# Four transformer layers on one core: the first model's output projection in two halves by rows, and the pieces of the modulation sums placed anew

## The chip, the cores and the metric

The kernel runs on one core of one Trainium2 chip. The metric is the device time of one execution in microseconds. TensorE is called PE here, VectorE DVE, ScalarE ACT, GpSimd POOL and SyncE SP, as in the profile.

## The reference

Two models run one after the other on 256 tokens of width 1024, each with two layers. Every layer adds a gated mixer and a gated feed-forward part to the tokens. The gates, shifts and scales of a layer are six vectors of width 1024, from one matrix product of a condition with a matrix of 1024 x 6144:

```python
c_act = jax.nn.silu(c)
mod = c_act @ ada_w[layer] + ada_b[layer]
sh_m, sc_m, gt_m, sh_f, sc_f, gt_f = jnp.split(mod, 6)
h = modulate(rms_norm(x, norm_mix_g[layer]), sh_m, sc_m)
x = x + gt_m * hybrid_mixer(h, ...)
h = modulate(rms_norm(x, norm_ffn_g[layer]), sh_f, sc_f)
x = x + gt_f * f(h)
# hybrid_mixer of the first model, after z = h @ w_in and the split into columns
rg_out = rg_lru(causal_depthwise_conv(rg_x), ...) * jax.nn.gelu(rg_gate)        # 512 wide
gla_out = rms_norm(gla_chunked(q, k, v, log_f)) * jax.nn.silu(g)                # 4 heads of 128
return jnp.concatenate([rg_out, gla_out], axis=-1) @ w_out
```

The feed-forward part is a gated unit of width 2816 in layer 0 of the first model and eight experts, two chosen for each token, in layer 1. The second model's mixer has a latent attention and a gated recurrent memory (mLSTM) with branch projections and an output projection; its feed-forward part has a short convolution. All is in float32.

## The kernel before

Tokens lie feature-major: x and h are eight blocks of 128 features by 256 tokens. Each engine runs one list of instructions written out by hand, and semaphores join them. Weights come in units of 1 MB through a ring of six slots; SP loads them in one fixed order (`unit_plan`), and the load of a unit waits until the unit that held its slot is used. A product of float32 precision is made of three in the rounded type float32r: the weights and the tokens are each split in a high part (ACT copies it with rounding, `high` in line 1429) and a low part (DVE subtracts, `low` in line 1950), and PE adds high x high, low x high and high x low in PSUM (`project_split`). The output projections and a few others are plain float32 matmuls (`project`), 128 instructions for the whole of `w_out`. The high part of the mixer's tokens is `mix_h_hi`. In the first model's mixer the eight input units are rgx 0 and 1, flow, q, k, v 0 and 1, gate 0 and 1, g 0 and 1; the second model's has vm 0 and 1 among them.

The modulation sums are made beside that. A layer's matrix is cut into 24 pieces of 128 rows by 2048 columns, 1 MB each. POOL loads a piece into a slot of `ada_in`; DVE multiplies it by its 128 conditions and adds it to one of the three accumulators `ada_acc` (`ada_piece`, line 1900, 2.35 us for a piece, 1.2 us for a first one). When all eight pieces of an accumulator are in, PE sums over partitions, one matmul with one column of ones for each 128 outputs (`modulation`, line 639): a layer has 48 such blocks, 16 in each accumulator, and each is two instructions. The third slot of `ada_in` is at the same time `mix_h_hi`, so that in layer 0 after the first eight pieces, in the last layer, and for the first pieces of the others, two slots are in use (`ada_plan`); the third is loaded only when the unit g 1 has been used.

Where a piece stands in DVE's queue is written by hand. In `mixer1` (line 2023) `late(li, a, b)` does a pieces in layer 0 and b in layer 1; those of layer 0 are the last 16 of its own 24, those of layer 1 belong to the second model's first layer, whose other 16 are done beside the experts. In `mixer2` the second model's last layer's pieces are done: 18 in the mixer, six in the convolution stage.

The end of `mixer1` on PE: the head products (o) into banks 6 and 7, the modulation columns, the sums of squares of the heads, and `project_out`, which waits for the whole concatenated input `ycat_ready`. DVE makes that input in h: the recurrent half as one product, each head half by a reciprocal, a scaling and two products with the silu of g. Then DVE adds bank by bank to x (`residual`, line 2154), ACT squares x, PE sums (`norm_sum`), ACT takes the root and DVE the reciprocal (`norm`), and the next stage begins. In layer 0 the low parts of the first feed-forward units w1 and w3 (`split_low`) stand on DVE before the residual, in `mixer2` those of u1 and u3.

## Time and profile before

| | |
|---|---|
| median of 3 runs | 2437.72 us (2433.67 to 2438.7) |
| the profiled execution | 2435.66 us |
| its span in the profile | 2433.9 us |
| PE busy, share | 2261.0 us, 93% |
| DVE busy, share | 1774.9 us, 73% |
| ACT busy, share | 1228.7 us, 50% |
| granted PE clock, mean | 0.95 |

The stages by the trace, in us from the start: start and first norm until 56, first mixer 56 to 230, feed-forward 230 to 421, second mixer 435 to 574, routing and experts 577 to 1415, second model's first mixer 1445 to 1720, convolution stage 1723 to 1925, last mixer 1940 to 2212, last convolution stage 2215 to 2413, output until 2434. A stage ends for the next when the last x is written and normed. A wait is shown with the instruction that ended it; a wait "by DVEq" or "ACTq" is one for a semaphore that the queue of that engine raised after an instruction had settled.

### The profile page before, as it was taken

What the parts mean: (1) busy time and instruction counts of PE and PEld (TensorE: products, weight loads), DVE (VectorE), ACT (ScalarE), POOL (GpSimd) and SP (SyncE); (2) the same over time, 40 slices, a digit from 0 to 9 for tenths busy, and PEclk for the clock granted to TensorE, in tenths of its full rate; (3) what the DMA queues carried; (4) which work ended last, traced back from release to release, by engine and by line L of the source; (5) the groups of instructions that cost most, each with busy time, mean ns of one, the idle gap of its engine ahead of it and who ended that gap; (6) DMA issues with size and microseconds to landing.
All of it is one profiled execution on the core that took longest, in us unless ns stands there. A gap on an engine that the chain in (4) does not pass through costs nothing.

```text
span 2433.9 us, 33478 instructions
## 1 busy us (share of the span) xinstructions
PE 2261.0 (93%) x13955; PEld 2020.0 (83%) x13955; DVE 1774.9 (73%) x1894; ACT 1228.7 (50%) x1338; POOL 55.2 (2%) x101
## 2 busy tenths in 40 slices
PE   3948999888999999999999989999999999999997
PEld 2847999877888888888888877878899988888997
DVE  5864876766898989999899856676677563556675
ACT  2612343633777677676767734522455444324553
POOL 1000000000000000000000000000000000000000
PEclk9968999977999999999999979989999898999998
DMA  8862987344999999999999925855466263234551
GB/s 279 272 247 70 339 301 277 123 144 185 355 353 379 355 370 369 352 378 357 371 368 352 355 66 146 278 189 191 156 211 203 73 159 104 87 133 138 181 192 51
DMA packets 338896, 578.55 MB, mean 238 GB/s; under 512 B 48083, under 2 KB 208811, under 8 KB 326451
## 3 DMA queue, kind: packets, MB, share of 16 engines
q1 hardware_dynamic: 324041, 474.36, 57.3%
q0 software_dynamic: 13824, 100.67, 10.9%
q8 instruction: 112, 1.84, 0.3%
q10 hardware_dynamic: 873, 1.31, 0.2%
q14 instruction: 46, 0.37, 0.1%
HBM read 575.26 MB, written 1.05 MB: 237 GB/s over the span
## 4 chain that ended last, share of the span: by engine, by line
PE 79%; DVE 10%; ACT 4%; DMA 3%; issue 2%; SPq 1%; DVEq 0%; ACTq 0%; POOL 0%
PE bank L557 78%; DVE w_low L1890 2%; ACT arena L1414 2%; DVE arena L1898 1%; DMA ring<-in_w_in 1%; DVE ada_acc L1898 1%; SPq L445 1%; DMA ada_in<-in_ada_w 1%; ACT L1414 1%; PE bank L1195 1%; DVE arena L1890 1%; ACT mix_hi L1414 1%; DVE arena L1980 1%; DVE arena L2331 1%; DVE arena L2091 1%
## 5 line engine op out<-in xcount | busy, mean ns | idle before, releaser
L1890 DVE TENSOR_TENSOR w_low<-ring,moe_w_hi 128x2048 fp32r<-128x2048 f32 x264 | 594.5, 2284 | 14.4 <-ACT moe_w_hi L1414 13.9
L1414 ACT ACTIVATE moe_w_hi<-ring 128x2048 fp32r<-128x2048 f32 x264 | 505.4, 1917 | 155.6 <-DMA ring<-in_moe_w 93.7
L557 PE MATMUL bank<-mix_h_hi,mix_hi 128*128 128x256 f32 (+2 forms) x848 | 255.7, 301 | 44.0 <-DVE w_low L1890 30.8
L557 PE MATMUL bank<-moe_w_hi,hx_hi 128*128 128x512 f32 (+1 forms) x768 | 285.2, 378 | 2.0 <-DVE hx_low L1890 2.0
L557 PE MATMUL bank<-moe_w_hi,hx_low 128*128 128x512 f32 (+1 forms) x768 | 284.1, 376 | 0.0
L557 PE MATMUL bank<-h_hi,w_hi 128*128 128x256 f32 x1056 | 263.5, 287 | 16.9 <-ACT h_hi L1414 11.3
L557 PE MATMUL bank<-h_hi,w_low 128*128 128x256 f32 x1056 | 262.4, 285 | 0.0
L557 PE MATMUL bank<-mix_h_hi,w_low 128*128 128x256 f32 (+2 forms) x848 | 250.1, 295 | 0.0
L557 PE MATMUL bank<-h_low,mix_hi 128*128 128x256 f32 (+2 forms) x848 | 244.7, 294 | 0.0
L1414 ACT ACTIVATE arena<-bank 128x512 f32<-128x512 f32 (+2 forms) x174 | 91.3, 525 | 265.3 <-PE bank L557 256.9
L1898 DVE SCALAR_TENSOR_TENSOR ada_acc<-ada_in,c_col,ada_acc 128x2048 f32<-128x2048 f32 x84 | 197.0, 2348 | 31.7 <-DMA ada_in<-in_ada_w 26.5
L557 PEld LDWEIGHTS bank<-h_hi,w_hi 128*128 128x128 f32 x1056 | 202.7, 192 | 18.7 <-issue 12.1
L557 PEld LDWEIGHTS bank<-mix_h_hi,mix_hi 128*128 128x128 f32 (+2 forms) x848 | 168.6, 199 | 53.1 <-issue 47.0
L557 PEld LDWEIGHTS bank<-h_hi,w_low 128*128 128x128 f32 x1056 | 204.1, 193 | 0.0
L557 PE MATMUL bank<-w_low,hx_hi 128*128 128x512 f32 (+1 forms) x768 | 194.1, 378 | 0.0
L1890 DVE TENSOR_TENSOR w_low<-ring,w_hi 128x2048 fp32r<-128x2048 f32 x66 | 148.8, 2289 | 38.9 <-ACT w_hi L1414 38.9
L557 PEld LDWEIGHTS bank<-moe_w_hi,hx_hi 128*128 128x128 f32 x768 | 145.1, 189 | 30.5 <-DVE hx_low L1890 2.2
L557 PEld LDWEIGHTS bank<-mix_h_hi,w_low 128*128 128x128 f32 (+2 forms) x848 | 169.0, 199 | 1.3
L557 PEld LDWEIGHTS bank<-moe_w_hi,hx_low 128*128 128x128 f32 x768 | 145.2, 189 | 28.0
L557 PEld LDWEIGHTS bank<-h_low,mix_hi 128*128 128x128 f32 (+2 forms) x848 | 165.2, 197 | 2.4 <-DVE h_low L1898 1.0
L1890 DVE TENSOR_TENSOR w_low<-ring,mix_hi 128x1024 fp32r<-128x1024 f32 (+2 forms) x128 | 138.7, 1126 | 35.4 <-ACT mix_hi L1414 27.8
L1414 ACT ACTIVATE w_hi<-ring 128x2048 fp32r<-128x2048 f32 x66 | 123.1, 1903 | 81.6 <-DMA ring<-in_ffn_w_up 63.2
(190 smaller groups left out, 4396.0 us busy)
## 6 DMA issues: line engine op xcount, KB each, us to landing
ring<-in_moe_w SPq DMA_DIRECT2D x264, 1024.0 KB, 6.2
ada_in<-in_ada_w POOLq DMA_DIRECT2D x96, 1024.0 KB, 7.5
ring<-in_w_in SPq DMA_DIRECT2D x56, 1024.0 KB, 5.4
ring<-in_ffn_w_up SPq DMA_DIRECT2D x44, 1024.0 KB, 7.1
ring<-in_ffn_w SPq DMA_DIRECT2D x33, 1024.0 KB, 5.8
ring<-in_ffn_w_down SPq DMA_DIRECT2D x22, 1024.0 KB, 4.9
ring<-in_w_out SPq DMA_DIRECT2D x16, 1024.0 KB, 5.3
ring<-in_w_br_mla SPq DMA_DIRECT2D x4, 1024.0 KB, 4.9
```

The costliest lines, as they stand in the source:

```text
L445: sp.dma_start(dst, src).then_inc(s["params"], 16)
L557: ins = nc.tensor.matmul(out, lhsT, rhs, start=start, stop=stop, skip_group_check=shared)
L1195: ins = nc.tensor.transpose(bank[2 * (q % 2)][:, i * P:(i + 1) * P], MS["hid"][:, i * P:(i + 1) * P], ident)
L1414: return nc.scalar.activation(out, in_, f, **kw)
L1890: return nc.vector.tensor_tensor(out, a, b, op)
L1898: return nc.vector.scalar_tensor_tensor(out, a, sc, b, op0, op1)
L1980: settle(nc.vector.reciprocal(region(2048, T), region(2304, T)))
L2091: settle(nc.vector.reciprocal(M1["rec"], M1["rec"]))
L2331: settle(nc.vector.reciprocal(M2["hstd"][:, sl], M2["hstd"][:, sl]))
```

## The change

- The first model's output projection is done in two halves by rows of `w_out`: for all four banks first the four blocks of the recurrent half (now in `gg`), then the four of the heads (now in `aa`). `ycat_ready` is raised three times, after the recurrent half and after each head half.
- The unit g 1 is projected behind the heads' products instead of before them; its silu stands behind the heads' square roots on ACT.
- `mix_h_hi` lies in the first accumulator instead of the third slot of `ada_in`. Three slots are in use throughout, and the pieces go accumulator by accumulator: 0, 1, 2 in the first model, 1, 2, 0 in the second.
- Pieces are placed anew. Layer 0's 16: 2, 1, 1 as before, then 2 behind the split of gate 1, 1 behind that of g 0, 3 behind the recurrent half, and 2, 2, 1, 1 beside the residual (before: 2, 1, 1, 2, 1, 6, 3). Layer 1 does 12 of the next 24 (2, 1, 1, 2, 1, 1 and 2, 1, 1, 0 beside the residual; before 3, 2, 2, 1 there), the experts 12 (before 16). In the second model's first mixer all 24: 4, six steps of the attention, five of the memory, 1, 1, and 2, 2, 2, 1 beside the residual.
- Modulation columns: in layer 0, 16 before the head sums and 16 after the norm's sum; in layer 1 all 32 before the mixer.
- Of the first two units of a mixer the second is split behind the norm's root (high part) and behind the tokens' low parts (low part). The high parts of vm 0 and 1 go behind later copies of ACT. The constant of the recurrence gate is made earlier.

The core of the diff; hunks are named by engine, and what is left out repeats these edits:

```diff
@@ placement of the buffers
-        ada_acc = sb("ada_acc", [P, ADA_SLOTS, SLOT])
-        ada_in = sb_at("ada_in", [P, ADA_SLOTS, SLOT])
+        ada_acc = sb_at("ada_acc", [P, ADA_SLOTS, SLOT])
+        ada_in = sb("ada_in", [P, ADA_SLOTS, SLOT])
...
-        mix_h_hi = rounded("mix_h_hi", [P, KB, T], "ada_in", 2 * SLOT)
+        mix_h_hi = rounded("mix_h_hi", [P, KB, T], "ada_acc")
...
-            return (layer, m % KB, m // KB) if layer == 0 else (layer, m // ADA_SLOTS, m % ADA_SLOTS)
+            return layer, m % KB, ((0, 1, 2) if layer < 2 else (1, 2, 0))[m // KB]
@@ gpsimd
-                slot, _, there = ada_places[n]
-                if there is not None:
-                    pool.wait_ge(s["ada_used"], there + 1)
-                if n in (ADA_PER_LAYER + 2, 2 * ADA_PER_LAYER + 2):
-                    pool.wait_ge(s["units_used"], plan[("g", n // ADA_PER_LAYER - 1, 1)][2] + 1)
+                slot = n % ADA_SLOTS
+                if n >= ADA_SLOTS:
+                    pool.wait_ge(s["ada_used"], n - ADA_SLOTS + 1)
@@ tensor
-            def gate_modulation():
+            def ffn_modulation():
+                need("ada_done")
                 fill(7)
-                modulation(7, 5 * KB, MODS)
+                modulation(7, 4 * KB, 5 * KB)
+                fill(0)
+                modulation(0, 5 * KB, MODS)
...
-                project_bank(("g", li, 1), 4)
-
                 need("scores_sb", 2)
                 need("states_sb")
...
+                project_bank(("g", li, 1), 4)
                 if li == 0:
                     need("ada_done")
-                fill(2)
-                modulation(2, 2 * KB, 3 * KB)
+                    fill(2)
+                    modulation(2, 2 * KB, 4 * KB)
                 need("headsq_sb", 2)
...
-                modulation(2, 3 * KB, MODS if li else 5 * KB)
-                project_out("wout", li, (2, 3, 5, 4))
+                gg = M1["gg"].rearrange("p (b t) -> p b t", b=4)
+                heads = M1["aa"].rearrange("p (b t) -> p b t", b=4)
+                banks = (2, 3, 5, 4)
+                need("ycat_ready")
+                for j, b in enumerate(banks):
+                    fill(b)
+                    arrive(("wout", li, j))
+                    w = slot_view(("wout", li, j), KB, 256)
+                    for i in range(2):
+                        for kb in range(4):
+                            mm(bank[b][:, i * T:(i + 1) * T], w[:, kb, i * P:(i + 1) * P], gg[:, kb, :],
+                               start=(i == 0 and kb == 0), stop=False, shared=True)
+                for j, b in enumerate(banks):
+                    w = slot_view(("wout", li, j), KB, 256)
+                    for hh in range(2):
+                        if j == 0:
+                            need("ycat_ready")
+                        for i in range(2):
+                            for head in (hh, hh + 2):
+                                mm(bank[b][:, i * T:(i + 1) * T], w[:, 4 + head, i * P:(i + 1) * P],
+                                   heads[:, head, :], start=False, stop=(head == 3), shared=True,
+                                   inc="wout_psum" if i and head == 3 else None)
+                    owed.append(1)
...
+            fill(7)
+            modulation(7, 2 * KB, MODS)
             mixer1(1)
@@ scalar: norm (for a mixer's two first units), mixer1, mixer2
-                for key in mixer:
-                    high(key)
+                if mixer:
+                    high(mixer[0])
                 need("norm_sum")
                 tell(func(region(2304, T), bank[1][:, 0:T], ACT.Sqrt, scale=1.0 / DM, bias=EPS), "norm_std", 1)
+                if mixer:
+                    high(mixer[1])
...
+                need("c8_ready")
+                func(small[:, 4:8], small[:, 4:8], ACT.Exp, scale=-1.0)
                 need("lf_abs")
...
-                need("c8_ready")
-                settle(func(small[:, 4:8], small[:, 4:8], ACT.Exp, scale=-1.0))
...
+                high(("g", li, 0))
                 need("rgchain_v")
...
-                for g, b, ahead in ((1, 6, ("km", li, 1)), (2, 7, ("vm", li, 0)), (3, 3, ("vm", li, 1))):
...
                 tell(func(M2["qr"], bank[5][:, :], ACT.Copy), "qr_sb", 5)
+                high(("vm", li, 0))
...
+                high(("vm", li, 1))
                 for half, b in enumerate((2, 4)):
@@ vector: mixer1
+                if li:
+                    modulation(1, 2 * KB, MODS, 7)
+                lam = v[:, PACK1["lam"]:PACK1["lam"] + 4]
+                tell(stt(small[:, 4:8], lam, -1.0, lam, ALU.mult, ALU.max), "c8_ready")
                 nc.vector.memset(M1["sc"], 0.0)
-                late(li, 2, 0)
+                late(li, 2, 2)
...
                 low(("k", li, 0))
-                late(li, 1, 0)
+                late(li, 1, 1)
                 low(("v", li, 0))
-                late(li, 1, 0)
+                late(li, 1, 1)
...
-                late(li, 2, 0)
                 low(("gate", li, 0))
...
-                late(li, 1, 0)
                 low(("gate", li, 1))
+                late(li, 2, 2)
+                low(("g", li, 0))
+                late(li, 1, 1)
...
-                low(("g", li, 0))
-                late(li, 6, 0)
...
-                late(li, 3, 0)
-                if li == 0:
-                    ada_finish(0)
...
-                need("outgate_sb", 2)
-                hh1 = h[:, 0:4, :].rearrange("p k t -> p (k t)")
-                settle(tt(hh1, M1["mu"], M1["gg"], ALU.mult))
+                tell(tt(M1["gg"], M1["mu"], M1["gg"], ALU.mult), "ycat_ready")
+                late(li, 3, 1)
+                if li == 0:
+                    ada_finish(0, 2)
+                    modulation(0, 2 * KB, 4 * KB, 2)
...
-                tell(ins, "ycat_ready")
-                modulation(li, 2 * KB, MODS if li else 5 * KB, 2)
+                    tell(ins, "ycat_ready")
                 if li == 0:
                     split_low("w", 0, 0)
-                residual((2, 3, 5, 4), 16, "wout_psum", (0, 0, 0, 0) if li == 0 else (3, 2, 2, 1))
+                residual((2, 3, 5, 4), 16, "wout_psum", lambda j: late(li, (2, 2, 1, 1)[j], (2, 1, 1, 0)[j]))
+                if li == 0:
+                    ada_finish(0)
@@ vector: mixer2, experts, convolution stage
-                    ada_next(1)
+                    if step < 6:
+                        ada_next(1)
...
                 gated_heads(1)
+                ada_next(1)
                 gated_attention(2, 5)
                 gated_attention(3, 1)
+                ada_next(1)
...
                 split_low("u", li, 0)
-                residual((0, 5, 3, 7), 16, "wout_psum")
+                residual((0, 5, 3, 7), 16, "wout_psum", lambda j: ada_next((2, 2, 2, 1)[j]))
+                if li == 0:
+                    ada_finish(3)
...
-                            if part == 1 and c in (0, 3):
+                            if part == 1 and (c == 0 or (c == 3 and e % 2 == 0)):
                                 ada_piece(next(pieces))
...
-                    if f % 3 == 1:
-                        for n in itertools.islice(pieces, 1):
-                            ada_piece(n)
```

## Rows read from the trace of the kernel before

**Rows 1.** first part of the page, busy time by engine.

```profile
...
PE 2261.0 (93%) x13955; PEld 2020.0 (83%) x13955; DVE 1774.9 (73%) x1894; ACT 1228.7 (50%) x1338; POOL 55.2 (2%) x101
...
```

**Rows 2.** busy time by stretch, then granted clock, DMA share, GB/s.

```profile
...
605.00:1405.00 800.00, 799.59 (x3905) 664.33 (x3906) 720.41 (x473) 563.64 (x402) 7.92 (x15) 1.00 0.99 359
153.60:166.60 13.00, 12.85 (x88) 12.06 (x88) 9.62 (x15) 0.62 (x2) 1.05 (x2) 0.89 0.47 166
1508.00:1522.00 14.00, 8.47 (x17) 4.12 (x18) 4.66 (x7) 7.69 (x12) 0.00 (x0) 0.76 0.13 41
...
```

**Rows 3.** waits of PE, 100 to 232 us: sum, times, longest.

```profile
...
PE bank L557 <- DVE w_low L1890: 23.6, 2, 18.4
PE bank L557 <- DVEq L1916: 7.1, 1, 7.1
PE bank L557 <- DVEq L1885: 6.1, 1, 6.1
...
```

**Rows 4.** groups of DVE, 104 to 190.3 us: busy, mean | idle before.

```profile
...
L1898 DVE SCALAR_TENSOR_TENSOR ada_acc<-ada_in,c_col,ada_acc 128x2048 f32<-128x2048 f32 x9 | 21.2, 2351 | 17.7 <-DMA ada_in<-in_ada_w 16.7 <-DVE arena L1898 0.7 <-DVE arena L1890 0.2
L1890 DVE TENSOR_TENSOR w_low<-ring,mix_hi 128x1024 fp32r<-128x1024 f32 x6 | 7.1, 1220 | 0.4 <-DVE arena L2100 0.2
L2141 DVE RECIPROCAL arena<-arena 128x512 f32<-128x512 f32 x2 | 6.7, 3349 | 0.0
...
```

**Rows 5.** waits of PE, 1445 to 2120 us.

```profile
...
PE bank L557 <- ACTq L1409: 11.6, 2, 5.9
PE bank L557 <- DVE w_low L1890: 7.7, 7, 3.0
PE bank L912 <- DVEq L1885: 6.7, 3, 4.0
...
```

**Rows 6.** DVE in order of time: start, length, what [idle before].

```profile
...
116.59 6.55 DVE L2091 RECIPROCAL arena<-arena 128x1024 f32<-128x1024 f32 x1
...
155.93 3.00 DVE L1898 SCALAR_TENSOR_TENSOR arena<-arena,small,bank 64x128 f32<-64x128 f32 x8
...
171.17 2.35 DVE L1898 SCALAR_TENSOR_TENSOR ada_acc<-ada_in,c_col,ada_acc 128x2048 f32<-128x2048 f32 x1 [6.75 <-DMA ada_in<-in_ada_w]
...
220.14 0.88 DVE L1898 SCALAR_TENSOR_TENSOR x<-bank,mod,x 128x256 f32<-128x256 f32 x2 [6.03 <-PE bank L557]
...
1716.28 0.88 DVE L1898 SCALAR_TENSOR_TENSOR x<-bank,mod,x 128x256 f32<-128x256 f32 x2 [6.03 <-PE bank L557]
...
```

**Rows 7.** groups of PE, 190.4 to 220.15 us.

```profile
...
L557 PE MATMUL bank<-h,ring 128*128 128x256 f32 x128 | 29.7, 396 | 6.1 <-DVEq L1885 6.1
...
```

**Rows 8.** GpSimd's issues in order of time.

```profile
...
162.25 0.53 POOL L535 DMA_DIRECT2D ada_in<-in_ada_w  x1 [10.95 <-DVE ada_acc L1898]
...
```

**Rows 9.** PE in order of time.

```profile
...
229.59 0.55 PE L557 MATMUL bank<-h_hi,w_hi 128*128 128x256 f32 x1 [4.35 <-ACT h_hi L1414]
...
435.03 0.55 PE L557 MATMUL bank<-mix_h_hi,mix_hi 128*128 128x256 f32 x1 [6.61 <-ACT mix_h_hi L1414]
...
```

**Rows 10.** groups of PE, 524 to 540.05 us.

```profile
...
L557 PE MATMUL bank<-const,ada_acc 128*128 128x1 f32 x64 | 12.5, 330 | 0.0
L557 PE MATMUL bank<-arena,const 128*128 128x512 f32 x4 | 3.8, 1096 | 0.0
```

**Rows 11.** busy time by stretch, as Rows 2.

```profile
...
529.50:539.50 10.00, 10.00 (x49) 10.00 (x47) 9.59 (x8) 0.60 (x1) 0.00 (x0) 0.50 0.12 42
421.30:424.80 3.50, 3.50 (x34) 3.50 (x33) 2.65 (x7) 1.33 (x3) 0.00 (x0) 1.00 0.56 168
...
```

**Rows 12.** groups of PE, 540.05 to 570.8 us.

```profile
...
L557 PE MATMUL bank<-h,ring 128*128 128x256 f32 x128 | 30.6, 405 | 0.4 <-issue 0.4
...
```

**Rows 13.** ACT in order of time.

```profile
...
1501.81 2.00 ACT L1414 ACTIVATE mix_hi<-ring 128x1024 fp32r<-128x1024 f32 x2 [10.08 <-DMA ring<-in_w_in]
...
1701.61 1.91 ACT L1414 ACTIVATE w_hi<-ring 128x2048 fp32r<-128x2048 f32 x1 [2.20 <-DMA ring<-in_ffn_w_up]
...
```

**Rows 14.** waits of PE, 2215.3 to 2413.1 us.

```profile
...
PE bank L557 <- DVE w_low L1890: 4.8, 3, 3.0
...
...
```

More of the change, by code:

```diff
@@ L207, in unit_plan @@
     return order, plan, earlier, split
-def ada_plan():
-    places, count, holder = [], [0] * ADA_SLOTS, [-3, -2, -1]
-    for n in range(4 * ADA_PER_LAYER):
-        layer, m = divmod(n, ADA_PER_LAYER)
-        two = (layer == 0 and m >= KB) or (layer in (1, 2) and m < 2) or layer == 3
-        slot = min(range(2 if two else ADA_SLOTS), key=lambda i: holder[i])
-        count[slot] += 1
-        places.append((slot, count[slot], holder[slot] if holder[slot] >= 0 else None))
-        holder[slot] = n
-    return places
 def two_blocks(nc, d, out):
     order, plan, earlier, split = unit_plan()
-    ada_places = ada_plan()
     MOE0, MOE_SLOT = plan[("moe", 0, 0)][2], plan[("moe", 0, 0)][0]
@@ L1555, in mixer1 @@
                 tell(ins, "rgchain_m")
-                high(("g", li, 0))
                 need("kend_psum")
@@ L1569, in mixer1 @@
                          "headsq_sb")
+                for half in range(2):
+                    need("headsum_psum")
+                    tell(func(M1["ostd"][:, half * 512:(half + 1) * 512], bank[half][:, :], ACT.Sqrt,
+                              scale=1.0 / P, bias=EPS), "headstd_sb", half)
                 for half, b in enumerate((5, 4)):
@@ L1573, in mixer1 @@
                          "outgate_sb", b)
-                for half in range(2):
-                    need("headsum_psum")
-                    tell(func(M1["ostd"][:, half * 512:(half + 1) * 512], bank[half][:, :], ACT.Sqrt,
-                              scale=1.0 / P, bias=EPS), "headstd_sb", half)
             def mixer2(li):
@@ L1601, in mixer2 @@
                      "cqstd", 0)
-                for g, b, ahead in ((1, 6, ("km", li, 1)), (2, 7, ("vm", li, 0)), (3, 3, ("vm", li, 1))):
+                for g, b in ((1, 6), (2, 7), (3, 3)):
                     conv_last_tap(li, v, qk, g, b)
-                    high(ahead)
+                    if g == 1:
+                        high(("km", li, 1))
                 need("m_rows")
@@ L1973, in split_h, with norm @@
                         ALU.add, ALU.subtract).then_inc(s["h_lo"], 1)
-            def norm(scale, out, inc, first=False, mixer=()):
-                for key in mixer:
-                    low(key)
+            def norm(scale, out, inc, columns=None, mixer=()):
+                if mixer:
+                    low(mixer[0])
                 need("norm_std")
                 settle(nc.vector.reciprocal(region(2048, T), region(2304, T)))
-                if first:
-                    modulation(0, 0, 2 * KB, 0)
+                if columns:
+                    modulation(*columns)
                 for kb in range(KB):
@@ L2537, in moe_dense @@
                 dve.sem_inc(s["moe_hid"], 4)
-                pieces = iter(range(2 * ADA_PER_LAYER + 8, 3 * ADA_PER_LAYER))
+                pieces = iter(range(2 * ADA_PER_LAYER + 12, 3 * ADA_PER_LAYER))
                 done = [0]
                 for e in range(EXPERTS):
-                    for j in range(2):
-                        ada_piece(next(pieces))
+                    for n in itertools.islice(pieces, 2):
+                        ada_piece(n)
                     for c in range(MOE_CHUNKS):
@@ L2565, in conv_ffn @@
                 t1, t2 = vcol[:, 4 + 2 * li, :], vcol[:, 5 + 2 * li, :]
-                pieces = iter(range(4 * ADA_PER_LAYER - 6, 4 * ADA_PER_LAYER) if li == 0 else ())
                 c0 = f0 - F0["conv0"]
@@ L2601, in _ @@
             start()
-            norm(scale_a[:, 0, :], h, "norm_mul", first=True, mixer=(("rgx", 0, 0), ("rgx", 0, 1)))
+            norm(scale_a[:, 0, :], h, "norm_mul", columns=(0, 0, 2 * KB, 0), mixer=(("rgx", 0, 0), ("rgx", 0, 1)))
             split_h(0, mix_h_hi, 0)
+            low(("rgx", 0, 1))
             rope()
             mixer1(0)
-            norm(scale_a[:, 1, :], h, "norm_mul")
-            modulation(0, 5 * KB, MODS, 7)
+            norm(scale_a[:, 1, :], h, "norm_mul", columns=(0, 4 * KB, 5 * KB, 7))
+            modulation(0, 5 * KB, MODS, 0)
             split_h(1, h_hi, 24)
@@ L2612, in _ @@
             split_h(2, mix_h_hi, 0)
+            low(("rgx", 1, 1))
             mixer1(1)
@@ L2620, in _ @@
             split_h(4, mix_h_hi, 0)
+            low(("cq", 0, 0))
             mixer2(0)
@@ L2627, in _ @@
             split_h(6, mix_h_hi, 0)
+            low(("cq", 1, 0))
             mixer2(1)
```

37 lines of the change are left out of this document (16 added, 21 removed).

## The prediction, before the changed kernel was run

> **What bounds the kernel now.** I began with the page's first part: PE is busy for 93% of the span, 173 us short of all of it, and DVE for 73% [rows 1]. The sum of busy time by stretch then says where those 173 us can lie. In the 800 us of the experts PE is busy for 799.59 us at a granted clock of 1.00, while DVE works for 720 us [rows 2]: fewer pieces there free DVE and nobody waits for it. So only PE's idle stretches and its half-clock stretches are to be had, and the view of waits names them. From 100 to 232 us, the first layer's mixer, PE waits 23.6 us for splits by DVE (one wait of 18.4), 7.1 us for the end of the pieces and 6.1 us for the gated heads [rows 3]: 37 us of some 130, and a short wait before the gate unit besides. In that stretch DVE's nine multiply-and-add pieces cost 21.2 us and another 16.7 us in which DVE itself waits for their transfers [rows 4]; they stand in the queue ahead of the split that the second g unit needs and ahead of the heads. In the second model PE waits 11.6 us in two equal waits for ACT, 6.7 us in three for the attention weights and 7.7 us for splits in the convolution stage [rows 5].
>
> **First layer, mixer: a gain of 28 us.** Pieces are re-placed, not saved: 16 stay between the first norm and the feed-forward stage. In the new queue 2 stand after the second gate split and 1 after the first g split. Before that point DVE loses about 1.4 us (the second rgx split, 2 x 1.2 us [rows 4], now stands behind the norm, which itself starts 1.2 us sooner) and wins 4.7 us from the two pieces taken out ahead of the gate split, so PE's short wait before the gate unit goes. DVE reaches the reciprocal chain at about the old moment, 116 us; the reciprocal alone is 6.55 us [rows 6], the chain 9.3, so 125.3. Then, with no piece in between, masks 1.7, split of g1 2.4 [rows 4], states 4.4 (3.0 of them the row at 155.93 [rows 6], the rest four copies ahead of it) and their settling: 134, where before it was 159. PE does the g0 unit meanwhile and idles for about 9 us, then does the heads' products and g1, which before, in the other order, took PE 12.9 us from 153.6 [rows 2], some 2 of it at half clock as now: 147.7 by my reckoning, states 134 and 13.7 us on. DVE in that time makes the first half of the concatenated input (2.5 + 2.4 + 1.2 us: 140.5) and three pieces, 147.7. PE then does 16 modulation columns, 3.6 us, and the head sums, 1.8 us: 153.3. The projection is 29.7 us for 128 instructions [rows 7]; its first half, 14.8 us, runs while DVE does the two head halves, each a reciprocal of 3.35 us [rows 4] and 1.5 us around it, after the square roots: 163.2. So PE would end near 183, not 220. But DVE is late then: two splits of w1 and w3 bring it to 169.6, and six pieces (14.1 us) and four residual pairs (1.1 us each) follow. Three transfers stand ready; the fourth must be fetched again. The slowest of these stood 8.9 us between issue, 162.25, and use, 171.17 [rows 8, 6], which would leave DVE waiting for 4 us over the tail; the other bound is nothing. I take 3, nearer the row. The last x is then written at about 191.3 against 220.14 + 0.9 [rows 6]. From there to the first matmul of the feed-forward stage was 8.6 us [rows 6, 9]; 16 columns on a slow PE stand before the scales now, 1.5 us more: 201.5 against 229.6, so 28. Bounds: 33 if no transfer is late, 20 if each of the last six costs what the longest did.
>
> For that transfer the Trainium skill, DMA: Bandwidth & Descriptors, section Bandwidth, gives 6.15 us for 1 MB from GpSimd's queue. By it DVE would hardly wait in this tail, the gain would be about 31 us, and with the other tail the sum 59 us in place of 55; the 8.9 us of [rows 8, 6] speak against it here, though they hold the issue too.
>
> **Second layer, mixer: 14 us.** All 32 modulation columns leave the end of the mixer, where 64 instructions of one column took 12.5 us and the head sums 3.8 us [rows 10], and stand behind the norm's sum, where PE idles for 6.61 us before its first projection [rows 9]. At a granted clock of 1.00, 34 such instructions fit in 3.5 us; from 529.5 to 539.5 us, at 0.50, there were 49 in 10 us [rows 11]. So 64 take from 6.6 to 13.1 us, and the start of the mixer moves from -1.5 us (PE does not go cold) to +7; I take +2.5, as the first half of them run warm. Then as in the first layer: states at about 514, products and g1 until 527.5, head sums until 529.3, projection 27.6 us at full clock: 556.9, against 570.7 before (30.6 us for it [rows 12]). The heads (534 and 539) are ready before PE has ended the first half at 543. Four pieces beside the residual fit into DVE's waits. Bounds 6 to 18 us. Without the split by rows this layer would start the projection at 539, so 10 of the 14 us hang on it; in the first layer DVE's tail swallows that difference.
>
> **Second model, both layers: 8 us each before the scores, 2 and 1 elsewhere.** ACT holds the copy that PE's rotation waits for behind the high part of a value unit whose weights arrive late: ACT idles 10.08 us for them [rows 13]. The diff puts those two high parts behind the copy; what they release is needed only 5 and 12 us later, so the wait that ends at 1513.53 goes. Each such wait is 5.8 us [rows 5], and the stretch behind it, 1508 to 1522, had a mean clock of 0.76 [rows 2], some 2.5 us of loss. That makes 8.3 in each layer; bounds 5 to 8.5. In the first of them the three pieces at the end of the attention loop go: the wait of 4.0 us [rows 5] has one piece of 2.35 us right in front of the normalisation, so 2.4 are saved. The norms gain 0.5 and 1.2 us. Together 11 and 10 us.
>
> **Tail of the second model's first layer: a loss of 11 us.** Seven pieces move behind the split of the first up units. That split waits for weights which SP may load only after the last branch unit is used: ACT begins u3's high part at 1701.61 [rows 13], DVE ends its low part at 1705.9. Before, four residual pairs followed, the last at PE's pace, from 1716.28 [rows 6] to 1717.2. Now 7 x 2.35 + 4 x 1.1 = 21 us follow on DVE, and a transfer that is 1 us late: 1728. Bounds 6 (part of the pieces hidden in a way I miss) to 16 us (three late transfers). What is given back: the convolution stage has no pieces, and its splits keep PE waiting 4.8 us in the last layer, which has none, against 7.7 us [rows 5, 14]: 3 us.
>
> **Hidden at nothing.** Four fewer pieces in the experts: PE's full queue covers them. The order j by j makes each piece wait for the one before it on its own engine, and DVE's settling is 0.2 us at most, between pieces that rarely touch. GpSimd's queue has three slots throughout and no longer waits for the g unit; only its transfers come earlier. The high part of the tokens changes place, not work. SP's queue is not changed.
>
> **Waits that are added.** PE's queue now stops three times for the concatenated input, for the product of the recurrent half and for each head half; behind the second stop stand all the second-half matmuls, and DVE's residual waits for those. In my times (140.5, 158 and 163 against 153, 168 and 168) none of the three is reached late. In the first layer PE also waits for two thirds of the pieces before its 16 columns, with the head sums behind it; that is 147.7, the moment at which g1 ends, and each us by which the three pieces are late there delays head sums, square roots and projection alike, though DVE's tail hides some 8 us of it. ACT waits for the second head half before it rounds w1 and w3; DVE's low parts stand behind that. ACT's exponential of the gate constant moves next to that of the log gate, so that two table loads go; what they held up is the gate split, already counted.
>
> **The sum.** 28 + 14 + 11 - 11 + 3 + 10 = 55 us. The profiled execution took 2435.66 us, its span 2433.9. So 2380.7, and for the shown runs, whose median lies 2 us above that execution, 2382 us. About 0.2%, 5 us, is what a measurement of this kernel tells from no change.
>
> **Rivals.** (1) PE's clock: the long row of one-column matmuls and the new 9 us gap before the heads' products cost double, with the projections beginning at half clock: +10, 2392 us, chance 0.14. For it speaks the clock of 0.50 in [rows 11]. (2) The tails: every refilled transfer takes 9 us or more because up to four ring loads go at the same time; first mixer 20, second model's tail -16: 2395 us, 0.13. (3) The value units' weights come too late for the new places as well, so PE stops at the values, not at the rotation: 11 to 16 us of the second model are lost, 2396 us, 0.07. (4) The gain is larger: no transfer late and no cold start of the second mixer, 33 + 18 + 11 - 10 + 3 + 10 = 65: 2372 us, 0.12. (5) Slower than before: one mechanism, the pieces' transfers. 16 pieces stay on DVE's path in the first mixer; if each waited 3.5 us more than my tails allow, the 55 us would be gone, and above it the kernel is slower: 2441 us at 3.7. Before, the nine pieces of [rows 4] made DVE wait 16.7 us, 1.9 each, with two slots in place of three; chance 0.02. (6) The split by rows does nothing, since PE reaches the first half only when the heads are done: 10 us of the second layer are lost, 2392 us, 0.05; the head sums, which PE must do first, leave 10 us for DVE, so little speaks for it. My forecast, 2376 to 2388, holds the rest, 0.47. The range 2367 to 2398 reaches to the first four cases. Faster 0.96, same 0.02, slower 0.02.
>
> **What would show it.** After: the wait of 18.4 us gone and one of about 9 us before the heads' products; DVE's last residual of layer 1 near 191 us and PE idle in front of it; the expert stage 40 us earlier and unchanged in length; no wait for ACT before the rotation; in the second model's first layer a PE wait of over 10 us before the convolution stage. Wrong if the chain before 116 us moves, or if weights, not pieces, set the tails.

## The result, and the profile after

| | before | after |
|---|---|---|
| median | 2435.69 us (4 runs) | 2395.49 us (4 runs, 2391.27 to 2400.01) |
| the profiled execution, its span | 2435.66, 2433.9 us | 2391.27, 2389.5 us |

The ratio is 0.9835, 95% interval 0.9811 to 0.9858: about 40 us faster, and 44.4 us between the profiled executions. Forecast were 2382 us (range 2367 to 2398) and 55 us. The direction and the places where the time moves were forecast; 11 us of the amount did not come between the profiled executions, and 15 by the medians. The profiled execution after is the fastest of its four, and no trace shows where the 4 us between the two figures lie. To see where the 11 us are missing, I cut both traces at the first matmuls of the stages. The last column is the prediction's term.

| stage, by PE | before | after | gained | forecast |
|---|---|---|---|---|
| start to the feed-forward stage | 229.6 | 206.8 | 22.8 | 28 |
| to the router (second mixer) | 348.0 | 337.2 | 10.8 | 14 |
| routing and experts | 842.1 | 840.9 | 1.2 | 0 |
| second model: norm, mixer, to its output projection | 268.7 | 259.5 | 9.2 | 11 |
| output projection to convolution stage | 34.7 | 46.6 | -11.9 | -11 |
| convolution stage and last mixer | 492.1 | 480.7 | 11.3 | 3 + 10 |
| last stage | 218.7 | 217.9 | 0.9 | 0 |

The page's first part shows the sum, where [rows 1] stood before: PE has lost 6 us of busy time and 38 us of idle time.

```profile
PE 2254.6 (94%) x13955; PEld 2016.7 (84%) x13955; DVE 1776.4 (74%) x1895; ACT 1223.7 (51%) x1334; POOL 53.7 (2%) x101
```

The waits of PE from 100 to 207 us answer to [rows 3]. Both waits for splits, the one for pieces and the one for the gated heads are gone; 7.3 us ahead of the heads' products stand in their place (the view names no releaser; PE's queue stands there for the states, which DVE settles at 134.7).

```profile
PE bank L542 <- issue: 7.3, 1, 7.3
PE bank L542 <- ACT arena L1417: 4.4, 3, 2.3
PE bank L542 <- ACTq L1414: 2.0, 1, 2.0
PE bank L542 <- DVEq L1895: 0.7, 1, 0.7
```

What the idle time costs is seen in PE's groups from 135 to 160.7 us and in the granted clock of the same stretch: the 40 small matmuls of the heads take 10.5 us at a clock of 0.50, and g 1 begins at 0.50 as well. Before, the 40 took 5.8 us, from 518.07 to 523.83.

```profile
L542 PE MATMUL bank<-arena 64*128 64x64 f32 (+1 forms) x40 | 10.5, 439 | 7.3 <-issue 7.3
...
L542 PE MATMUL bank<-const,ada_acc 128*128 128x1 f32 x32 | 4.4, 272 | 0.0
L542 PE MATMUL bank<-arena,const 128*128 128x512 f32 x4 | 3.8, 1096 | 0.0
```

```profile
135.00:145.50 10.50, 10.50 (x41) 9.14 (x41) 9.72 (x10) 0.60 (x1) 0.96 (x1) 0.50 0.01 2
145.50:152.70 7.20, 7.20 (x51) 7.20 (x51) 2.35 (x1) 0.60 (x1) 1.12 (x3) 0.80 0.91 341
```

PE in order of time: the same ten microseconds again in the second mixer, then the two starts that answer to [rows 9] and to the convolution stage. In the wait of 6.56 us PE stands for ACT's square of x, and ACT for DVE, which has pieces to do first.

```profile
135.00 10.52 PE L542 MATMUL bank<-arena 128*128 128x128 f32 x40 [7.28 <-issue]
...
206.80 0.58 PE L542 MATMUL bank<-h_hi,w_hi 128*128 128x256 f32 x1 [0.67 <-DVEq L1895]
...
489.99 10.52 PE L542 MATMUL bank<-arena 128*128 128x128 f32 x40 [7.28 <-issue]
...
1681.48 2.08 PE L542 MATMUL bank<-arena,const 128*128 128x256 f32 x4 [6.56 <-ACT arena L1417]
...
1690.92 0.55 PE L542 MATMUL bank<-h_hi,w_hi 128*128 128x256 f32 x1 [3.46 <-ACT h_hi L1417]
```

DVE in order of time, first mixer and second model's first: it idles 9.14 us before the heads and 9.71 us before the split of u1, and in both tails works through pieces while PE has ended. Only one transfer is late in the first tail, by 1.68 us.

```profile
157.04 0.18 DVE L1898 TENSOR_TENSOR mod<-bank,vcol 128x16 f32<-128x16 f32 x1 [9.14 <-PE bank L542]
...
186.52 2.35 DVE L1906 SCALAR_TENSOR_TENSOR ada_acc<-ada_in,c_col,ada_acc 128x2048 f32<-128x2048 f32 x1 [1.68 <-DMA ada_in<-in_ada_w]
...
195.70 0.87 DVE L1906 SCALAR_TENSOR_TENSOR x<-bank,mod,x 128x256 f32<-128x256 f32 x2
...
1655.80 2.29 DVE L1898 TENSOR_TENSOR w_low<-ring,w_hi 128x2048 fp32r<-128x2048 f32 x1 [9.71 <-ACT w_hi L1417]
...
1683.65 0.87 DVE L1906 SCALAR_TENSOR_TENSOR x<-bank,mod,x 128x256 f32<-128x256 f32 x2
```

### The profile page after: what moved, and what is told of

The parts are those of the page before. It is cut to its first block, busy times and chain, and to the rows that moved or that the text cites. A ratio compares the mean times of both kernels' runs of the same rounds, so it can differ in the third digit from the quotient of the medians.

```text
span 2389.5 us, 33477 instructions
## 1 busy us (share of the span) xinstructions
PE 2254.6 (94%) x13955; PEld 2016.7 (84%) x13955; DVE 1776.4 (74%) x1895; ACT 1223.7 (51%) x1334; POOL 53.7 (2%) x101
## 4 chain that ended last, share of the span: by engine, by line
PE 84%; DVE 8%; ACT 3%; DMA 2%; issue 2%; SPq 1%; DVEq 0%; ACTq 0%; POOL 0%; POOLq 0%
PE bank L542 82%; ACT arena L1417 1%; DVE w_low L1898 1%; SPq L432 1%; DMA ring<-in_w_in 1%; DVE ada_acc L1906 1%; PE bank L1196 1%; DVE arena L1906 1%; DMA ada_in<-in_ada_w 1%; DVE arena L1898 1%; ACT mix_hi L1417 1%; DVE arena L2344 1%; DVE arena L2101 1%; DVE h L1906 0%; DMA ring<-in_ffn_w_up 0%
## 5 line engine op out<-in xcount | busy, mean ns | idle before, releaser
L1898 DVE TENSOR_TENSOR w_low<-ring,moe_w_hi 128x2048 fp32r<-128x2048 f32 x264 | 594.4, 2285 | 14.6 <-ACT moe_w_hi L1417 14.2
L1906 DVE SCALAR_TENSOR_TENSOR ada_acc<-ada_in,c_col,ada_acc 128x2048 f32<-128x2048 f32 x84 | 197.3, 2348 | 19.5 <-DMA ada_in<-in_ada_w 12.6
L542 PEld LDWEIGHTS bank<-mix_h_hi,mix_hi 128*128 128x128 f32 (+2 forms) x848 | 167.0, 197 | 22.8 <-issue 14.1
L1906 DVE SCALAR_TENSOR_TENSOR arena<-bank,vcol,arena 128x255 f32<-128x255 f32 (+3 forms) x252 | 111.0, 481 | 79.2 <-ACT arena L1417 75.1
L542 PEld LDWEIGHTS bank<-moe_w_hi,hx_low 128*128 128x128 f32 x768 | 145.1, 189 | 27.9
```

Source lines behind the costliest of these rows:

```text
L542: ins = nc.tensor.matmul(out, lhsT, rhs, start=start, stop=stop, skip_group_check=shared)
L1898: return nc.vector.tensor_tensor(out, a, b, op)
L1906: return nc.vector.scalar_tensor_tensor(out, a, sc, b, op0, op1)
```

## Experiments

Two theories for the missing 11 us. **Clock:** PE idles before the heads' products and pays for it at half clock. **Transfers:** refilled pieces come late. Rivals for single terms: the split by rows does nothing; the edit of vm 0 and 1 does nothing. Ratios below are to the kernel before, run on the same chip.

### e1: the output projection not split by rows

```diff
-                need("ycat_ready")
+                need("ycat_ready", 3)
                 for j, b in enumerate(banks):
...
-                        if j == 0:
-                            need("ycat_ready")
```

> The changed kernel, but PE waits for the recurrent half and both head halves before the first matmul of the output projection; the rest is unchanged. If the split by rows hides the two head halves, as the prediction has it: in the first layer the projection starts at 170.2 in place of 160.4 us and the last x comes 4 to 5 us later (DVE's tail hides the rest), in the second it starts at about 519.6 in place of 509.3, 10 us later: 14 to 15 us slower than the changed kernel, a ratio to the kernel before near 0.989. If the split does nothing, because PE reaches the projection only when the heads are done: no difference, 0.983. If DVE's tail hides the whole of it in the first layer: 10 us, 0.987.

Measured 2409.11 us, ratio 0.9907 (0.9888 to 0.9927), some 17 us above the changed kernel's ratio, where 14 to 15 were expected. The waits of PE from 100 to 575 us show the two stops:

```profile
PE bank L542 <- DVEq L1891: 19.8, 2, 10.2
```

From first projection to feed-forward stage the first layer took 156.3 us in place of 150.6, and the second, to the router, 142.2 in place of 129.1. The second costs 13 us, not 10, since PE runs slower behind the wait: the 128 matmuls took 30.1 us at a mean clock of 0.93, in place of 27.8 at 1.00. The split does what it was given, and a little more.

### e3 and e5: the value units' edit alone, on the kernel before

```diff
@@ scalar (e3 and e5)
-                for g, b, ahead in ((1, 6, ("km", li, 1)), (2, 7, ("vm", li, 0)), (3, 3, ("vm", li, 1))):
+                for g, b in ((1, 6), (2, 7), (3, 3)):
...
                 tell(func(M2["qr"], bank[5][:, :], ACT.Copy), "qr_sb", 5)
+                high(("vm", li, 0))
...
+                high(("vm", li, 1))
@@ vector (e5 only)
-                low(("vm", li, 0))
                 conv_taps(v, qk, 3, 3)
-                low(("vm", li, 1))
+                low(("vm", li, 0))
...
+                low(("vm", li, 1))
                 need("atok_psum")
```

> The kernel before, with one edit of the change alone: the high parts of the units vm 0 and vm 1 on ACT behind the copies of the rotated query part and of the values, in both layers of the second model. By the prediction each layer wins 5.8 us of wait and 2.5 us of half clock behind it: 16 to 17 us faster than before, a ratio of 0.993. If only the waits go and the clock behind them stays low: 11 to 12 us, 0.995. If the weights come too late for the new places as well, PE waits at the values instead and 0 to 5 us are won, 0.998 to 1.000.

e3: 2436.03 us, ratio 1.0014 (1.0001 to 1.0026). All three expectations missed: not even the wait's 11 us came. From the first projection to the next stage the first of the two layers took 280.7 us in place of 277.7, the second 272.1 in place of 274.7. The waits of PE from 1500 to 1560 us and DVE's order of time say why for the first:

```profile
PE bank L557 <- ACTq L1411: 6.5, 1, 6.5
PE bank L557 <- DVEq L2376: 3.8, 1, 3.8
```

```profile
1506.74 2.36 DVE L1893 TENSOR_TENSOR w_low<-ring,mix_hi 128x1024 fp32r<-128x1024 f32 x2 [4.54 <-ACT mix_hi L1414]
1509.02 2.68 DVE L1901 SCALAR_TENSOR_TENSOR arena<-bank,vcol,arena 128x255 f32<-128x255 f32 x6
```

The low part of vm 0 stands on DVE ahead of the last convolution taps (the six at 1509.02), which the rotation waits for as well. With the high part later on ACT, DVE waits for it in ACT's stead, and again at vm 1 (8.5 us). My prediction speaks only of ACT; the diff has a second half.

> The kernel before with the change's whole edit of the units vm 0 and vm 1: their high parts later on ACT, as in e3, and their low parts later on DVE too, vm 0 behind the last convolution taps and vm 1 behind the rotated queries. Reading of e3: with ACT's half alone, DVE stood at the low part of vm 0 ahead of the taps that the rotation needs, PE waited 3.8 us for DVE instead of 5.8 for ACT, and 6.5 us more behind it, so nothing was won. If that is the whole reason, this kernel wins what the prediction gave the edit: no wait before the rotation in either layer, 16 to 17 us faster than before, ratio 0.993. If the weights of vm are late for the new places too: PE waits at the value products, 0 to 6 us won, 0.998 to 1.000. If only the waits go and not the half clock behind them: 11 to 12 us, 0.995.

e5: 2418.32 us, ratio 0.9932 (0.9917 to 0.9948): the expected 16 to 17 us, of which the traces have 6.5 in the first layer and 9.8 in the second. No wait stands before the rotation. The rival (weights late for the new places) falls.

### e4: g 1 ahead of the heads' products again

```diff
                 project_bank(("g", li, 0), 5)
+                project_bank(("g", li, 1), 4)
                 need("scores_sb", 2)
...
-                project_bank(("g", li, 1), 4)
                 if li == 0:
```

> The changed kernel, with the unit g 1 projected ahead of the heads' products again, in the 7.28 us in which PE now idles before them, in both layers of the first model. If that idle time and the low clock behind it are what made the stretch from the states to the head sums longer than forecast: g 1 takes 6 to 7 us in the gap, the heads' products 6 us in place of 10.5. First layer: the modulation columns are held until 147.9 us by the three pieces, so head sums, heads and tail come 4 to 5 us sooner; second layer: head sums 8 to 9 us sooner. 12 to 14 us faster than the changed kernel. If the products are slow for another reason (their own form, small matmuls), they take 10.5 us here too: 8 to 9 us faster. If the place of g 1 does not matter, since DVE's work sets the start of the head sums: no difference.

Measured 2380.13 us, ratio 0.9779 (0.9756 to 0.9803), 13 to 14 us below the changed kernel's ratio. The first layer took 147.0 us in place of 150.6, the second 119.9 in place of 129.1. PE's groups from 479.7 to 491.3 us and their clock:

```profile
L542 PE MATMUL bank<-arena 64*128 64x64 f32 (+1 forms) x40 | 5.8, 285 | 0.0
L542 PE MATMUL bank<-mix_h_hi,mix_hi 128*128 128x256 f32 x16 | 4.6, 287 | 1.8 <-DVE w_low L1898 1.8
```

```profile
479.70:491.30 11.60, 11.58 (x88) 10.77 (x88) 10.79 (x21) 0.60 (x1) 0.00 (x0) 1.00 0.61 211
```

The same 40 matmuls, right behind work in place of behind 7.28 us of nothing, take 5.8 us in place of 10.5, at a clock of 1.00 in place of 0.50. Their form alone is not the reason. The 9.2 us of the second layer add up from the rows: 5.5 are idle time (7.28 less 1.78), 6.0 are the products and g 1 at full clock (5.8 and 6.0 us in place of 10.5 and 7.3), and 2.4 go back, since the head sums now wait 0.7 us for ACT's squares and take 3.5 us at 0.56 in place of 1.9. In the first layer g 1 went at a mean clock of 0.77 (7.5 us) behind the same 1.8 us of idle time, and PE then waited 3.1 us for the pieces ahead of the columns.

### e9: g 1 first, but behind the idle time

e4 changes two things, the idle time and what stands first behind it. [rows 2] has a case that made me doubt the idle time alone: behind 18.4 us of it, g 1 and then the products took 12.9 us together.

```diff
                 need("scores_sb", 2)
                 need("states_sb")
+                project_bank(("g", li, 1), 4)
...
-                project_bank(("g", li, 1), 4)
```

> The changed kernel with the unit g 1 right behind the wait for the states and ahead of the heads' products: PE's idle time of 7.3 us stays as it is (e4 closed it), only the order of the two pieces of work behind it changes. e4 left open whether the idle time alone makes the stretch slow or which work stands first behind it. If the idle time alone does: g 1 and the products together take 17.8 us here too, as in the changed kernel, and the time is the same, ratio 0.983. If the order does, the wide matmuls of g 1 bringing the clock back before the small ones begin: g 1 takes about 7.3 us and the products 5.8, as in the kernel before, where both took 12.9 us behind an idle time of 18.4; 4.7 us less in the second layer, and in the first 4.7 too, up to the head sums: 8 to 10 us faster than the changed kernel, ratio 0.979 to 0.980.

Measured 2391.99 us, ratio 0.9839 (0.9818 to 0.9859): as the changed kernel. The two idle times are there, as PE's waits from 100 to 512 us show, and the products are not slow behind them:

```profile
PE bank L542 <- DVEq L2126: 13.1, 2, 7.3
```

```profile
145.80 5.76 PE L542 MATMUL bank<-arena 128*128 128x128 f32 x40
```

In the stretch itself the order counts: g 1 and the products take 14.2 us in the first layer (137.4 to 151.6) and 13.5 in the second, where the changed kernel took 17.7 (135.0 to 152.7). It is not seen in the whole: of the 3.5 us in the first layer 2 are left at the feed-forward stage (148.9 us in place of 150.6 to 151.0), and the stage behind it took 211.1 us in place of 208.1. In the second layer 0.6 of the 4.3 us are left: g 1 starts 1.0 us later (g 0 ahead of it took 7.5 us in place of 6.0), and the head sums give 2.4 back as in e4 (0.7 us of wait, 3.5 us at 0.55), the projection 0.3. Both simple readings fail: the order is worth some 4 us for each place locally and nothing in the whole. What e4 wins needs the idle time filled, and of its 9.2 us in the second layer the idle time is about half, the clock the other.

### e2 and e7: pieces ahead of the split of u1 and u3

```diff
@@ vector, mixer2 (e2 and e7)
+                ada_next(3)
                 split_low("u", li, 0)
-                residual((0, 5, 3, 7), 16, "wout_psum", lambda j: ada_next((2, 2, 2, 1)[j]))
+                residual((0, 5, 3, 7), 16, "wout_psum", lambda j: ada_next(1))
@@ gpsimd (e7 only)
+                if n == 92:
+                    slot3, count3, _ = plan[("u3", 0, 0)]
+                    pool.wait_ge(slot_full[slot3], 16 * count3)
```

> The changed kernel, with three of the seven pieces at the end of the second model's first mixer put ahead of the split of the first up units, where DVE idles for 9.7 us, and the other four one by one beside the residual (in place of 2, 2, 2, 1 behind the split). If the pieces on DVE's path are the loss of 10 to 11 us in that tail: the last x comes at 1674 to 1675 us in place of 1684.5, and the kernel is 8 to 10 us faster than the changed one. If the pieces' transfers set the tail: the three that stand in the slots are done, but the four behind them wait 7 us each for a slot, so 0 to 3 us are won. If the convolution stage takes back what starts earlier, because its weights are loaded no sooner: its waits for splits, 4.6 us now, grow by the gain.

e2: 2385.72 us, ratio 0.9817 (0.9797 to 0.9838), an interval that overlaps the changed kernel's. The edit can act only from the mixer's output projection on, so I measure it from there to the first matmul of the convolution stage:

| kernel | us |
|---|---|
| before | 34.7 |
| changed; again in c1, e1, e4, e9 | 46.6; 46.9 to 47.1 |
| e2 | 44.6 |
| e7 | 37.7 |
| e6 | 40.6 |
| e8 | 37.9 |

e2 won 2.0 to 2.5 us there, not 8 to 10. (From the norm's start it took 300.7 us against 306.1, but 2.1 of these 5.4 are the norm, 25.8 us in place of 27.9 at a clock of 0.70 in place of 0.62, and 1.3 lie in the mixer; the edit touches neither.) That is the size of the second theory, 0 to 3, but not its reason: DVE waited for none of the pieces. ACT, in order of time, rounds u1 and u3:

```profile
1650.17 1.91 ACT L1417 ACTIVATE w_hi<-ring 128x2048 fp32r<-128x2048 f32 x1 [29.76 <-DMA ring<-in_ffn_w_up]
1661.55 1.91 ACT L1417 ACTIVATE w_hi<-ring 128x2048 fp32r<-128x2048 f32 x1 [9.47 <-DMA ring<-in_ffn_w_up]
```

Not the pieces but the weights are late: u3, issued by 1644.3, is used at 1661.5, 17 us later; in the changed kernel it was 9.3 (1647.9 to 1657.3). The Trainium skill, DMA: Bandwidth & Descriptors, section Bandwidth, has 6.15 us for the transfer of 1 MB issued from GpSimd. These loads are issued by SP and timed to their use, and neither is that short: the one of 9.3 us had other loads beside it too, 368 GB/s in all. GpSimd's queue in e2, and below it in e7:

```profile
1645.63 0.53 POOL L520 DMA_DIRECT2D ada_in<-in_ada_w  x1 [11.49 <-DVE ada_acc L1906]
1648.09 0.53 POOL L520 DMA_DIRECT2D ada_in<-in_ada_w  x1 [1.94 <-DVE ada_acc L1906]
1650.55 0.53 POOL L520 DMA_DIRECT2D ada_in<-in_ada_w  x1 [1.93 <-DVE ada_acc L1906]
```

> The kernel of e2 (three pieces ahead of the split of u1 in the second model's first layer), and GpSimd issues the three loads that refill their slots only when the load of u3 has landed. In e2 u3's load took from about 1644 to 1661.5 us, beside those three at 371 to 404 GB/s; in the changed kernel it was there at 1657.3, from 1648. If the refills take the weights' share of the transfers: ACT rounds u3 at about 1654 in place of 1661.5, and although the pieces behind it come 3 to 5 us after DVE is free, the last x is at 1674 to 1675 in place of 1679.2: 4 to 5 us faster than e2. If u3 is late for another reason, such as its slot: ACT rounds it at 1661 as before, and the pieces come later: 5 to 6 us slower than e2.

```profile
1659.24 1.57 POOL L523 DMA_DIRECT2D ada_in<-in_ada_w  x3 [20.49 <-DMA ring<-in_ffn_w_up]
```

e7: 2385.62 us, ratio 0.9803 (0.9787 to 0.982). u3 is rounded at 1658.71, 10.0 us behind its issue, and the stretch takes 37.7 us: 6.9 less than e2, 9 less than the changed kernel. So the loss in this tail was pieces on DVE's path, and a DVE that asks for them earlier starts transfers that delay the next weights. Over the whole kernel the intervals of e2 and e7 overlap: e7's profiled execution gave 3 us back in the stage of the first feed-forward part (211.1 against 208.1 us) and 7.6 in the last mixer (272.0 against 264.5), which the edit does not touch; more of that below.

### c1, e6 and e8: the changed kernel again, and a version that beats it

> The changed kernel without any edit, on the chip of the three kernels beside it, as their measure: its ratio to the kernel before was 0.9835, interval 0.9811 to 0.9858, so 0.983 to 0.985 again.

c1: 2393.55 us, ratio 0.9831 (0.9814 to 0.9849), as before. e6 is e4 with both tails re-placed:

```diff
@@ vector, mixer1
                     modulation(0, 2 * KB, 4 * KB, 2)
+                    late(li, 1, 0)
...
                 if li == 0:
+                    late(li, 1, 0)
                     split_low("w", 0, 0)
-                residual((2, 3, 5, 4), 16, "wout_psum", lambda j: late(li, (2, 2, 1, 1)[j], (2, 1, 1, 0)[j]))
+                residual((2, 3, 5, 4), 16, "wout_psum", lambda j: late(li, 1, (2, 1, 1, 0)[j]))
@@ vector, mixer2 (split_low takes the units to split)
+                ada_next(3)
+                split_low("u", li, 0, (0,))
+                ada_next(2)
+                split_low("u", li, 0, (1,))
+                residual((0, 5, 3, 7), 16, "wout_psum", lambda j: ada_next((0, 1, 1, 0)[j]))
```

> The changed kernel with g 1 ahead of the heads' products, as in e4, and both tails re-placed. First layer: of the six pieces behind the splits of w1 and w3 one goes into DVE's idle time ahead of the first head half, one into the 2 us ahead of the splits, and four stand one by one beside the residual: the last x at PE's pace, 5 to 6 us sooner than in e4 (about 186 in place of 191.8 us). Second model's first layer: three pieces ahead of the split of u1, two between the splits of u1 and u3, where DVE waited 9 us in e2 for u3's weights, and two beside the residual: last x some 9 us sooner than in the changed kernel. If pieces on DVE's path set both tails: 26 to 30 us faster than the changed kernel. If the refilled transfers set them: DVE waits for pieces ahead of the head halves and ahead of u3, each such wait moves the path itself, and no more than e4's 12 to 14 us are won. If u3's weights arrive later still, since more pieces are fetched beside them: 18 to 22 us.

e6: 2365.49 us, ratio 0.971 (0.9691 to 0.973), 28 us below c1 on the same chip. The first mixer took 138.9 us (e4: 147.0), and no transfer of its tail is waited for; the second mixer took 120.5 us, and the tail of the second model's first layer 40.6, with 3.3 us in which DVE stands for the high part of u3. The feed-forward stage now begins at:

```profile
193.96 0.58 PE L542 MATMUL bank<-h_hi,w_hi 128*128 128x256 f32 x1 [2.88 <-ACT h_hi L1417]
```

e8 joins the two: e6's first layer, e7's tail with the held refills, and

```diff
-                late(li, 3, 1)
+                late(li, 1, 1)
                 if li == 0:
                     ada_finish(0, 2)
+                    late(li, 2, 0)
```

> The kernel of e6 with the tail of the second model's first layer as in e7 (three pieces ahead of the splits, their refills held until u3's weights have landed, four pieces one by one beside the residual), and in the first layer the release of the 16 modulation columns behind the first of the three pieces in place of behind all three. In e7 the stage from that mixer's first projection to the convolution stage took 268.2 us, in e6 271.7. If the held refills are worth the same here: 3 to 4 us, and the earlier columns 1.4: 4 to 5 us faster than e6, ratio to the kernel before 0.969. If e7's shorter stage came from the clock of that execution: 1 to 2 us, 0.9705.

e8: 2360.52 us, ratio 0.9708 (0.9687 to 0.9729): not told apart from e6. Both local expectations came: from the first projection to the convolution stage it took 268.3 us against 271.7, and the first mixer 137.6 against 138.9. Yet the second mixer took 123.8 us against 120.5 and the stage ahead of it 211.2 against 208.1. There the 64 modulation columns, moved by the change to this place, run while PE waits for nothing; first the changed kernel, then e8, columns as [rows 2]:

```profile
406.10:414.80 8.70, 8.70 (x65) 8.70 (x63) 8.03 (x17) 5.58 (x11) 0.00 (x0) 0.79 0.00 1
```

```profile
393.60:404.70 11.10, 11.10 (x66) 11.10 (x64) 10.45 (x19) 5.58 (x11) 0.00 (x0) 0.61 0.00 1
```

## Why the prediction was right in direction and 11 to 15 us too large

- **First layer, 28 forecast, 22.8 measured.** DVE's order came as worked out: chain at 116.8 (116), states 134.7 (134), recurrent half 141.3 (140.5), pieces 147.9 (147.7). The step that failed is "147.7 by my reckoning, states 134 and 13.7 us on": I put 2 us of half clock into it, and the idle time of 7.28 us was followed by 10.5 us for the heads' products and 7.3 for g 1, so PE got to the columns at 152.6. A second term was too small: columns and head sums had 5.6 us in the forecast and took 8, because the head sums (1.8 us in it) went at 0.50 behind the columns and took 3.8, as they had in [rows 10]. They ended at 160.6 in place of 153.3; of these 7.3 us 1 is the later start, 4 are products and g 1, 2.4 columns and head sums. All behind it shifted: last x at 196.6 against 191.3. e4 gives back 4 us here with the one order. DVE waited 1.7 us for transfers where I had 3, between bounds of 4 and nothing.
- **Second layer, 14 forecast, 10.8 measured.** Of the 2.5 us for moved columns 2.7 came. The mixer itself is 13.5 us shorter in place of 16.5, again the products after 7.28 us idle (17.8 us with g 1, where 13.5 to 13.7 were forecast); e4 gives 9.2 us back. The split by rows was worth 10 in the forecast and 13 in e1.
- **Second model before the scores.** The mechanism is shown by e5: both waits go, some 16 us over two layers. In the first, 9.2 in place of 11: the mixer alone gave 11.4, but the norm, forecast 0.5 shorter, took 27.9 us in place of 25.8 (27.8 or 25.8 in the other kernels, at a mean clock of 0.62 or 0.70).
- **Tail of the second model's first layer, -11 forecast, -11.9 measured**, with PE's waits behind the output projection at 9.2 us (6.6 + 1.8 + 0.8), where one of over 10 was forecast. DVE waited 3.0 us for transfers, forecast 1.
- **Convolution stage and last mixer, 13 forecast, 11.3 measured.** The sum is near by luck, its two parts are not. The convolution stage with the norm behind it gave 7.1 us, where 3 and the norm's 1.2 were forecast: PE's waits for splits there fell from 7.7 to 4.8 us as said, the wait of 1.1 us before the mixer went, and the norm's part was 3.0 us shorter (12.6 in place of 15.6). The last mixer gave 4.2 us of some 9. Its wait of 5.8 us is gone too, but it took 270.5 us where e5, with this edit alone, took 264.9; the same mixer went in 264.5 us in e2 and e8.
- **Hidden at nothing.** The experts took 0 to 1 us less, as said.

Of my rivals the first, PE's clock, comes nearest, with its place, its sign and about its size: 10 us, 2392. By the rows above the clock cost 4 us behind each gap, 2 in the first head sums and 2 in the norm. It is shown stretch by stretch and not in the whole: e9, which takes away the 4 us behind each gap alone, was no faster. I gave it 0.14 and priced the stretch by [rows 2], 153.6 to 166.6, where g 1 went first; e9 comes near that row for its order (13.5 and 14.2 us against 12.9), but the change has the other order, and small matmuls behind the gap went at 0.50 to the last. The split's rival and the value units' rival fell (e1, e5). The transfers' rival did not hold for the change (1.7 us in one tail, 3.0 in the other). But once DVE asks earlier, loads beside each other do delay one another, as e2 and e7 show, and then it is the weights that come late.

Left open: why the same long runs of one-column matmuls go at one clock in one kernel's execution and at another in the next. The stage with the 64 moved columns took 208.1 us in six kernels and 211.1 in three (e7, e8, e9), 205.4 before the move, and the last mixer 264.4 to 272.1 us in kernels that do not differ there. Single profiles carry this spread. The medians of e6 and e8 differ by no more than it, and e9's 4 us for each place can be lost in it too.

## What to carry to other kernels

A gap in PE's queue is priced with the work that follows it: before a unit of work is moved out of a gap, ask what will run at the low clock behind it, and put ready work in; a row of the same work in another order is no price for it. An edit of a split value has a side in each engine's queue, and moving one side alone moves the wait. When an engine that is not the bound becomes faster, look at which loads it sets free and which load on the path they will then stand beside.

## What the runs showed of the chip

- An idle time of 7.28 us on PE was followed by 10.5 us of small matmuls at a granted clock of 0.50 throughout. One of 1.8 us in e4 was followed by g 1 at 1.00 in the second layer and at a mean of 0.77 in the first, and the small ones went at 1.00 in both. With the wide matmuls of g 1 first, behind 5.8 and 7.3 us of idle time, the small ones behind them took 5.8 us again (e9).
- The granted clock fell while 64 one-column matmuls ran, with PE busy throughout: its mean was 0.79 over 8.7 us in the changed kernel and 0.61 over 11.1 us in e8. The 16 wide matmuls of the norm's sum just ahead of them, themselves behind 32 such columns at 1.00, had a mean of 0.68.
- A weight load of 1 MB took 17 us from issue to use beside three piece loads (e2, 365 GB/s from 1642 to 1664 us), 10.0 us when those were held back (e7), and 9.3 us in the changed kernel.
